# Keys of the later heads transposed by transfers, and a ring of four tiles for the gated outputs

## The reference

```python
q = rotary(q...); k = rotary(k...) * (DK_HEAD ** -0.5)
def step(S, qkv):
    s = jnp.einsum('bihd,bjhd->bhij', qc, kc) * intra_dec[None]
    o = jnp.einsum('bhij,bjhe->bihe', s, vc)
    o = o + jnp.einsum('bihd,bhde->bihe', qc, S) * inter_dec[None, :, :, None]
    S = S * carry_dec[None, :, None, None] + jnp.einsum('bjhd,bjhe->bhde', kc * upd_dec[...], vc)
o = o * lax.rsqrt(jnp.mean(o * o, axis=-1, keepdims=True) + RMS_EPS)
r = (jax.nn.silu(g) * o) @ w_ret_out
c = (cb * conv3(cc * cx)) @ w_conv_out
m = sigmoid(gr) * r + sigmoid(gc) * c
h = layer_norm(ALPHA * x + m @ w_o); y = layer_norm(ALPHA * h + (silu(a) * b) @ w_down)
```

## Time and profile before

| | us |
|---|---|
| median of three runs | 1597.03 |
| the profiled execution, its own time | 1602.78 |
| its span on the slowest core (core 0) | 1601.7 |
| spans of the eight cores | 1592.0 to 1601.7 |
| PE busy, of the span | 98% |
| DVE, ACT, POOL busy | 50%, 28%, 16% |

### The profile page before, as it was taken

How to read it: one execution, slowest core, us unless ns; L and a number is a source line. 1 busy time by engine, 2 the same in 40 slices (tenths; PEclk the granted TensorE clock), 3 DMA queues, 4 the chain that set the end, 5 groups by cost and what they waited for, 6 DMA issues and landing times.

```text
span 1601.7 us, 27096 instructions; the slowest of 8 cores (1592.0 to 1601.7 us)
## 1 busy us (share of the span) xinstructions
PE 1566.6 (98%) x9033; PEld 867.6 (54%) x9118; DVE 804.5 (50%) x1510; ACT 444.7 (28%) x875; POOL 258.4 (16%) x468
## 2 busy tenths in 40 slices
PE   5999999999999999999999999999999999999997
PEld 2555556655664445555665566444455566556653
DVE  3566672255222856668424622275666842472226
ACT  1555511123110055551111311004555211141100
POOL 2122210111110222221101111022222110021102
PEclk9999999999999999999999999999999999999999
DMA  9976696569863699669656986369996976478522
GB/s 188 159 99 97 96 208 96 83 121 192 148 97 53 126 199 196 119 119 203 98 93 108 193 141 99 53 132 191 208 139 120 164 138 112 85 145 140 101 45 79
DMA packets 87782, 207.45 MB, mean 130 GB/s; under 512 B 32992, under 2 KB 34656, under 8 KB 87648
## 3 DMA queue, kind: packets, MB, share of 16 engines
q0 software_dynamic: 40752, 149.70, 59.8%
q1 hardware_dynamic: 46320, 54.96, 12.6%
q10 hardware_dynamic: 576, 1.05, 0.2%
HBM read 329.11 MB, written 19.96 MB: 218 GB/s over the span
## 4 chain that ended last, share of the span: by engine, by line
PE 90%; DVE 5%; issue 2%; DMA 1%; POOL 1%; DVEq 0%; ACT 0%; ACTq 0%; POOLq 0%
PE P L950 19%; PE P L554 15%; PE P L834 12%; PE P L755 11%; PE P L1007 9%; PE P L856 8%; PE P L519 8%; PE P L708 2%; PE P L642 2%; PE P L913 2%; DVE sb_stat L882 1%; DVE sb_RA L916 1%; DMA sb_xT<-xT 1%; POOL sb_stat L892 1%; PE P L638 1%
## 5 line engine op out<-in xcount | busy, mean ns | idle before, releaser
L950 PE MATMUL P<-sb_R,sb_W 128*128 128x384 bf16 x2112 | 345.2, 326 | 0.0
L950 PEld LDWEIGHTS P<-sb_R,sb_W 128*128 128x128 bf16 x2112 | 206.3, 98 | 135.7
L188 POOL DMA_DIRECT2D sb_W<-wb x278 | 152.7, 553 | 753.6 <-PE P L950 281.0
L554 PE MATMUL P<-sb_W,sb_xT 128*128 128x512 bf16 x1076 | 254.8, 382 | 1.5 <-issue 0.4
L755 PE MATMUL P<-sb_xT,sb_W 128*128 128x384 bf16 x1152 | 198.4, 329 | 0.0
L554 PEld LDWEIGHTS P<-sb_W,sb_xT 128*128 128x128 bf16 x1104 | 107.4, 98 | 127.5 <-issue 12.2
L519 PE MATMUL P<-sb_xT,sb_W 128*128 128x384 bf16 x768 | 143.9, 333 | 17.1 <-DVE sb_W L1046 10.3
L755 PEld LDWEIGHTS P<-sb_xT,sb_W 128*128 128x128 bf16 x1152 | 112.3, 99 | 76.5 <-issue 1.8
L849 DVE TENSOR_TENSOR sb_scr<-P,sb_scr 128x384 f32<-128x384 f32 x96 | 53.2, 556 | 193.5 <-PE P L856 161.9
L834 PE MATMUL P<-sb_xT,sb_W 128*128 128x384 bf16 x768 | 133.1, 326 | 0.0
L856 PE MATMUL P<-sb_RA,sb_W 128*128 128x384 bf16 x768 | 132.6, 326 | 0.0
(11 more groups left out here) (97 smaller groups left out, 1636.2 us busy)
## 6 DMA issues: line engine op xcount, KB each, us to landing
sb_W<-wb POOLq DMA_DIRECT2D x278, 512.0 KB, 10.8
sb_xres<-xp SPq DMA_DIRECT2D x16, 512.0 KB, 13.2
sb_xres<-sret SPq DMA_DIRECT2D x16, 512.0 KB, 15.0
ss_o<-sb_xres SPq DMA_DIRECT2D x16, 512.0 KB, 6.8
yp<-sb_RA SPq DMA_DIRECT2D x15, 512.0 KB, 4.2
sb_lnp<-lnp SPq DMA_DIRECT2D x12, 512.0 KB, 10.8
sb_xT<-xT POOLq DMA_DIRECT2D x5, 768.0 KB, 14.2
sb_cst<-cs SPq DMA_DIRECT2D x6, 384.0 KB, 10.8
```

The lines of the kernel that those rows point to most:

```text
L188: (self.E[q].dma_start_transpose if turn else self.E[q].dma_start)(out=o, in_=i).then_inc(self.dsem[key], 16)
L554: S.pe([(lambda kc=kc: nc.tensor.matmul(P[b][:, :], xtile(s, kc, t), ws[kc // 4][:, kc % 4, :], start=(kc == 0), stop=(kc == 7)), [wc_(s, ...
L950: S.pe([(lambda kc=kc: nc.tensor.matmul(P[b][:, 0:n], w[:, kc, ji * 128:ji * 128 + 128], hT(kc, c0, c0 + n), start=(kc == 0), stop=(kc == 7)),
```

## The change

Keys of heads 1 to 3 in stage 0 and of heads 2 and 3 in stages 1 and 2 are no longer transposed on PE. A transposing transfer from SP's queue takes three tiles (128 x 768 bf16) out of `kT` into `kraw`, a single buffer behind the ring in the same space as the LayerNorm parameters; it is issued at the end of tile 1 (tiles 0 to 2) and of tile 4 (tiles 3 to 5) of the head before. `k_tr` then is only the ACT copy with the decay, from `kraw`. For a transfer to read three tiles in one run, `kT` is laid out tile by tile. To make room for `kraw`, the ring of gated outputs has four tiles in place of eight.

```diff
-        kT = [V3(SET[i], 3072, 2, TS, BF16) for i in range(2)]
+        kT = [V3(SET[i], 3072, NT, 256, BF16) for i in range(2)]
...
-        ogd = V3(LNP, 0, 8, 512, BF16)
+        ogd = V3(LNP, 0, 4, 512, BF16)
+        kraw = V3(LNP, 4096, NT, 256, BF16)
...
-            tt(dst(0, c0, c0 + n), r[0], r[1], ALU.subtract, [rc[0], rc[1]], [dst.c(0, c0, c0 + n)])
-            tt(dst(1, c0, c0 + n), r[2], r[3], ALU.add, [rc[2], rc[3]], [dst.c(1, c0, c0 + n)])
+            for hf, (x, y, op) in enumerate(((0, 1, ALU.subtract), (2, 3, ALU.add))):
+                d, view, dc = dst(hf)
+                tt(d, view(r[x]), view(r[y]), op, [rc[x], rc[y]], [dc])
...
+        def k_sent(s, h):
+            return h > (0 if s == 0 else 1)
+
+        def k_send(s, h, t0, m=3):
+            if k_sent(s, h):
+                ks = kT[h % 2]
+                S.dma("sp", f"kt{t0}", [(kraw.full[:, t0:t0 + m, :].rearrange("p a (u b) -> p (a u) b", u=2), ks.full[:, t0:t0 + m, :].rearrange("p a b -> p (a b)"))],
+                      reads=[ks.c((t0, t0 + m))], writes=[kraw.c((t0, t0 + m))], turn=True)
+
         def k_tr(s, h, t):
+            if k_sent(s, h):
+                S.op("act", lambda: nc.scalar.activation(out=kp(t % 2), in_=kraw(t), func=AF.Identity, scale=vec(kind, h, h + 1)),
+                     reads=[kraw.c(t), vec.c()], writes=[kp.c(t % 2)])
+                return
...
         def og_slot(h, t):
             if t in BYDMA:
-                return ogd, (4 * h + BYDMA.index(t)) % 8
+                return ogd, BYDMA.index(t)
...
                     run(fill[t])
+                    if h + 1 < H and t in (1, 4):
+                        k_send(s, h + 1, 0 if t == 1 else 3)
```

More of the change, by code:

```diff
@@ L534, in rope, with dst @@
             t1, t2 = P[b1][:, 0:n], P[b2][:, 0:n]
-            dst = (kT if which == "K" else qT)[h % 2]
+            m = n // 128
+            t0 = c0 // 128
+            def dst(hf):
+                if which == "Q":
+                    return qT[h % 2](hf, c0, c0 + n), lambda a: a, qT[h % 2].c(hf, c0, c0 + n)
+                o = hf * 128
+                return (kT[h % 2]((t0, t0 + m), o, o + 128), lambda a: a.rearrange("p (a b) -> p a b", a=m), kT[h % 2].c((t0, t0 + m), o, o + 128))
             def tt(o, a, b, op, rd, wr):
@@ L593, in gate @@
             wdone(s, ("G", h, 0), ("G", h, 1))
-        def k_tr(s, h, t):
+        def k_sent(s, h):
[5 more added lines that the diff above has]
+                      reads=[ks.c((t0, t0 + m))], writes=[kraw.c((t0, t0 + m))], turn=True)
+        def k_tr(s, h, t):
+            hs = h % 2
+            kind = tiles[s][t]["kind"]
+            if k_sent(s, h):
+                S.op("act", lambda: nc.scalar.activation(out=kp(t % 2), in_=kraw(t), func=AF.Identity, scale=vec(kind, h, h + 1)),
+                     reads=[kraw.c(t), vec.c()], writes=[kp.c(t % 2)])
+                return
             b = bank()
-            hs = h % 2
             pb = P[b][:].bitcast(BF16)
[L601 to L604, removed]
+            S.pe([(lambda hf=hf: nc.tensor.transpose(pb[:, hf * 128:(hf + 1) * 128], kT[hs](t, hf * 128, hf * 128 + 128), idb(0)),
+                   [kT[hs].c(t, hf * 128, hf * 128 + 128), idb.c()]) for hf in range(2)], [f"P{b}"])
             S.op("act", lambda: nc.scalar.activation(out=kp(t % 2), in_=pb[:, 0:256], func=AF.Identity, scale=vec(kind, h, h + 1)),
@@ L612, in scores @@
             tt = (t * 128, t * 128 + 128)
-            S.pe([(lambda hf=hf: nc.tensor.matmul(P[b][:, 0:128], kT[hs](hf, *tt), qT[hs](hf, *tt), start=(hf == 0), stop=(hf == 1)),
-                   [kT[hs].c(hf, *tt), qT[hs].c(hf, *tt)]) for hf in range(2)], [f"P{b}"])
+            S.pe([(lambda hf=hf: nc.tensor.matmul(P[b][:, 0:128], kT[hs](t, hf * 128, hf * 128 + 128), qT[hs](hf, *tt), start=(hf == 0), stop=(hf == 1)),
+                   [kT[hs].c(t, hf * 128, hf * 128 + 128), qT[hs].c(hf, *tt)]) for hf in range(2)], [f"P{b}"])
             kind = tiles[s][t]["kind"]
```

## The result

The changed kernel takes 1609.38 us (median of 12 runs) beside 1599.38 us for the kernel before (12 runs on the same chip). The ratio, from runs without the disturbance of a die, is 1.005, with a 95% interval of [1.003, 1.007]: slower. I had forecast 1595.0 us, within 1591.3 to 1600.5 us, and put 0.11 on slower.

A forecast was written before the change was run, and what follows sets the result against it. PE, busy 98% of the span, was taken as the bound. Gain of 4.6 us less 2.7 us for the ring gave -1.9 us on the median of 1597.03, told as 1595.0 us, range 1591.3 to 1600.5 us.

The forecast's parts named there:

- What is removed: Key transposes on PE: 42 of 72 tiles leave at 0.11 us each, 4.6 us off PE's path (4.2 to 5.0).
- What is added at no cost: ACT copy out of SBUF, key rope in three runs, 14 more transfers on SP: 0 us.
- What the shorter ring adds: Head 1, tile 1, stages 1 and 2: `gated` waits for head 0's transfer; PE loses 2.7 us (0 to 4.4).
- 16 readings: Waits of `gated` read on eight cores and two stages: all above zero, 0.6 to 3.6 us, mean 2.15 us.
- the reserve: At `gated` of head 1, tile 1: DVE's delay that PE takes without loss, 1.4 us.
- Do the keys arrive in time? Cost 0: Head 2's first keys land 3.8 us before their copy in stage 1, stage 2 similar; stage 0 has about 22 us.
- rival (b): Head 2's first keys, stages 1 and 2, land over 12.1 us after issue; slower from about 16 us; chance 0.10.
- The reserve of 2.8 us: Behind head 2's first key copy: ACT's casts end 2.8 us before PE needs them, so PE pays from 15 us.
- (a): The ring's wait in stages 1 and 2 is swallowed and the whole gain arrives: 1592.4 us; chance 0.22.
- (c): Gain eaten whole: ring wait of 3.6 us in both stages on the slowest core, or small waits: 1597 us; chance 0.12.
- The sum: Core 0's profiled execution: 1602.78 - 4.6 + 2.7 = 1600.9 us; the difference, -1.9 us, applied to the median.

## Why the prediction was wrong

- **What is removed** was right: 84 instructions fewer, and 4.7 us between the milestones for 4.6. The prediction did not see that 0.7 us of it is lost again behind them.
- **What is added at no cost** was right: copies at 0.50 us, rope unchanged at 546 ns, layout 1.0007.
- **What the shorter ring adds**: place and cause were right in all 16 readings, the reserve was 1.1 to 1.2 us for 1.4. On the mean core of after it is 2.6 us, for the 1.6 us that the prediction gave it; on core 0 it is 2.2 us for 2.7. It was mis-sized for long waits: past 3.7 us the half-rate matmuls behind the stop are added. Alone, on the slowest core, the ring costs 5.8 us.
- **"Do the keys arrive in time? Cost 0" is the step that failed.** It took the time of two more blocks from a landing in the quiet, 0.6 us a block. In the jam six blocks took 35.0 us. It called stage 0 safe because "nothing holds SP". In the kernel before that was so: none of the 128 issues of transposing transfers in stage 0, on eight cores, takes more than 2.3 us. In after 28 of 176 take more than 5 us, and the key transfer of 75.41 held SP for 10.76 us. The prediction set the margin against today's landings, although the change itself puts 14 more transfers, 11200 packets more on a queue of 46320, on the resource whose speed it took for granted. In stages 1 and 2 its reading was right for the profiled execution of after: the first keys of head 2 landed after 5.2 to 10.1 us on all eight cores, with 9.7 us or more at hand. The later experiments found rival (b)'s own place as well, as a matter of chance. The reserve of 2.8 us given there would make 4.1 us of the wait of 6.94 us, which cost 5.0.
- **Rivals (a) and (c)** fell: the ring's wait was swallowed in only one of the 16 readings (core 1, stage 2, 1.10 us), and on the mean core of after it did not eat the gain.
- **The sum** was one core's. With eight cores and a metric of the slowest, a delay that comes to one core in three is paid nearly always (an estimate from the 15 spans of 40: (25/40)^8, 2%, for a kernel of which no core is struck), while the gain is only what the unluckiest core keeps.

The Trainium skill (VectorE: DVE Perf Modes, "Rules for kernel authors") says to transpose on TensorE where PSUM will do. Every version here agrees: 0.055 us a block on PE, and 1.0033 or more for any version whose keys go by transfer and are used. The Trainium skill (Advanced Engine Details and Errata, section "X-Bar Transpose (TRN2)") says that transposing transfers are as fast as regular ones. For three tiles of keys the quickest landings come near that: 2.1 us for the plain copy, 2.7 us for the transposing one. What the issue costs differs: a plain copy held SP for 0.5 to 1.6 us in stage 0, a transposing one of the same bytes for up to 15.18 us in the stretch shown above.

What stays open: why a core falls into the jam at one time and not at another (in one execution one core loses 17 us and another none), whether it starts in the queue of the transposes or in that of the weights, and whether PE's unnamed stops are late instructions.

## What to carry to other kernels

Before work is moved to transfers, price them at their landing in the busiest stretch where they will run, not in the quiet, and count what they add to the queue that is already slow there. Where the metric is the slowest of several cores, ask how often a delay strikes any of them: a sure gain of 3 us on each core is lost to a delay of 5 to 17 us on one. Reading each core by milestones shows at once which gain arrived and what each stop really cost.

## What the runs showed of the hardware

- Transposing transfers beside a stream of weights slow down tenfold: from 20 ns a packet and landings of 2.4 to 7 us to some 200 ns a packet and landings of up to 35 us, weights slowed with them from 5.4 to 26.8 us. Values between occur too (landings of 12 to 20 us). A core can stay so for tens of us.
- The issue of a transposing transfer holds SP for 1.2 to 2 us in the quiet and for 9 to 17 us in the jam, so that what is queued behind it is issued late (26.14 us for three).
- A packet of the program's instructions took 9.7 us in the jam, for 1.0 us, and PE stood still for 7.21 us around it.
- Behind a stop of 4.51 us eight matmuls took 3.62 us in place of 1.89, at 1.2 GHz for 2.4, and the granted clock of the 20 us from 110 us on was 0.83; a late key that left PE idle for 2.6 us cost 5.0 us.
